# Splits, copies and requests in other orders at seven places of a two-block transformer kernel on one core

## The reference

```python
proj = x @ w_in
q_dsa, c_kv, q_idx, k_idx, w_idx, q_m, k_m, v_m, ga, gb = jnp.split(proj, points, axis=-1)
c_kv = rms_norm(c_kv, kv_norm_g)
k_idx = layer_norm(k_idx, idx_k_norm_g, idx_k_norm_b)
o_a = dsa_attention(q_dsa, c_kv, q_idx, k_idx, w_idx, w_uk, w_uv)
o_b = moba_attention(q_m, k_m, v_m)
merged = sigmoid(ga + b0) * (o_a @ w_o_dsa) + sigmoid(gb + b1) * (o_b @ w_o_moba)
x = layer_norm(ALPHA * x + merged @ w_out)
x = layer_norm(ALPHA * x + mem_cross_attention(x, mem, w_q, w_kv, w_o))
x = layer_norm(ALPHA * x + swiglu(x, w_ffn_in, w_ffn_out))
```

```python
u = depthwise_conv_centred(h2 @ w_up, w_conv, b_conv)
a, v = jnp.split(u, 2, axis=-1)
x = x + gate2 * ((silu(a) * v) @ w_down)
```

## Time and profile before

| | us |
|---|---|
| median of 3 runs (lowest, highest) | 2565.04 (2564.85, 2565.62) |
| the profiled execution | 2564.12 |
| its span, first to last instruction | 2562.5 |
| TensorE busy | 2496.3 (97%) |
| VectorE busy | 1672.0 (65%) |
| ScalarE busy | 1246.3 (49%) |
| GpSimd busy | 106.0 (4%) |
| mean granted TensorE clock | 0.991 |

### The profile page before, as it was taken

How to read it: one execution, slowest core, us unless ns; L and a number is a source line. 1 busy time by engine, 2 the same in 40 slices (tenths; PEclk the granted TensorE clock), 3 DMA queues, 4 the chain that set the end, 5 groups by cost and what they waited for, 6 DMA issues and landing times.

```text
span 2562.5 us, 45817 instructions
## 1 busy us (share of the span) xinstructions
PE 2496.3 (97%) x17896; PEld 2332.3 (91%) x17896; DVE 1672.0 (65%) x2081; ACT 1246.3 (49%) x1582; POOL 106.0 (4%) x149
## 2 busy tenths in 40 slices
PE   7999999999989999999999979999899999999998
PEld 7799999998979999999988878988899999997886
DVE  5564675557867777777777775575666666665556
ACT  4444564444555444444444554544555555554444
POOL 0000000000100000000122000000000000000000
PEclk9999999999999999999999989999999999999999
DMA  7455445569646888888978735446355555555553
GB/s 275 163 183 192 164 147 181 185 230 355 261 167 260 337 343 331 341 334 339 362 287 325 262 121 214 169 158 218 132 195 196 194 188 192 195 198 186 190 196 115
DMA packets 81632, 581.92 MB, mean 227 GB/s; under 512 B 9260, under 2 KB 9420, under 8 KB 11408
## 3 DMA queue, kind: packets, MB, share of 16 engines
q1 hardware_dynamic: 64800, 462.98, 49.3%
q0 software_dynamic: 14464, 104.23, 10.5%
q10 hardware_dynamic: 2288, 13.59, 1.4%
HBM read 578.64 MB, written 2.12 MB: 227 GB/s over the span
## 4 chain that ended last, share of the span: by engine, by line
PE 95%; DVE 3%; ACT 1%; issue 1%; DMA 0%; ACTq 0%; DVEq 0%
PE ps L2005 60%; PE ps L2048 23%; PE ps L2009 7%; PE ps L2072 2%; PE ps L1961 1%; PE ps L2300 0%; DVE xn L1520 0%; PE ps L2146 0%; DVE res L1525 0%; PE ps L2179 0%; PE ps L2191 0%; DVE wlo L1133 0%; DMA xT<-in_xt 0%; DVE res L1664 0%; DVE res L1671 0%
## 5 line engine op out<-in xcount | busy, mean ns | idle before, releaser
L1133 DVE TENSOR_TENSOR wlo<-raw,whi 128x1024 fp32r<-128x1024 f32 x860 | 1041.5, 1227 | 673.8 <-ACT whi L591 670.6
L591 ACT ACTIVATE whi<-raw 128x1024 fp32r<-128x1024 f32 x860 | 901.5, 1061 | 965.6 <-PE ps L2005 596.1
L2005 PE MATMUL ps<-xhi,whi 128*128 128x256 f32 x4176 | 1158.7, 277 | 8.7 <-issue 5.8
L2005 PE MATMUL ps<-xhi,wlo 128*128 128x256 f32 x4176 | 1152.6, 276 | 0.0
L2005 PE MATMUL ps<-xlo,whi 128*128 128x256 f32 x4176 | 1152.4, 276 | 0.0
L2005 PEld LDWEIGHTS ps<-xhi,whi 128*128 128x128 f32 x4176 | 787.3, 189 | 10.9 <-issue 6.7
L2005 PEld LDWEIGHTS ps<-xlo,whi 128*128 128x128 f32 x4176 | 787.2, 188 | 0.4
L2005 PEld LDWEIGHTS ps<-xhi,wlo 128*128 128x128 f32 x4176 | 786.8, 188 | 0.0
L1185 DVE SCALAR_TENSOR_TENSOR ada<-ada,cb 128x2048 f32<-128x2048 f32 x96 | 219.4, 2286 | 4.5 <-DMA ada<-in_w_ada 4.4
L2048 PE MATMUL ps<-whi,dhi 128*128 128x512 f32 x640 | 197.8, 390 | 4.1 <-DVE conv L1899 4.1
L2048 PE MATMUL ps<-whi,dlo 128*128 128x512 f32 x640 | 197.4, 390 | 0.0
(11 more groups left out here) (350 smaller groups left out, 2100.3 us busy)
## 6 DMA issues: line engine op xcount, KB each, us to landing
raw<-in_stream SPq DMA_DIRECT2D x437, 1024.0 KB, 4.8
ada<-in_w_ada POOLq DMA_DIRECT2D x96, 1024.0 KB, 6.8
xT<-in_xt SPq DMA_DIRECT2D x4, 512.0 KB, 10.6
mem_part<-in_memt ACTq DMA_DIRECT2D x2, 1024.0 KB, 7.1
res<-in_x ACTq DMA_DIRECT2D x1, 2048.0 KB, 13.7
gamma<-in_ln_g ACTq DMA_DIRECT2D x2, 1024.0 KB, 11.1
beta<-in_ln_b ACTq DMA_DIRECT2D x2, 1024.0 KB, 15.1
gate_row<-gate_store POOLq DMA_DIRECT2D x2, 1024.0 KB, 6.1
```

Of the source, the lines that this page charges most:

```text
L591: act.activation(whi[:, h % 4], raw[g % 4][:, 1024 * half:1024 * half + 1024], ACT.Copy)\
L1133: dve.tensor_tensor(wlo[:, h % 4], raw[g % 4][:, 1024 * half:1024 * half + 1024], whi[:, h % 4].bitcast(F32), ALU.subtract).then_inc(lo_re ...
L2005: ins = pe.matmul(o, w[:, k, P * m:P * m + P], a(kt), start=begins and n == 0 and m % 2 == 0, stop=ends and n == 2, skip_group_check=True)
```

## The change

Nothing that is computed changes, and no instruction of work is added or removed, but for table loads; the order does.

1. SP waits for a landing before each request of the first tiles: for tile 0's first half ahead of the second quarter of x, and then for the landing before last. ScalarE requests the two constants after it has split tile 1.
2. Tile 6 is split by ScalarE and VectorE ahead of the copies of the transposed latents.
3. ScalarE's attention loop is written out, head by head.
4. TensorE waits for the last two heads only after three half tiles of the first gate product.
5. The first half of `o_mem`'s second tile is split ahead of the heads' copies, and the square root's table is loaded after the last split.
6. In `out2` that table is loaded ahead of the last turn.
7. The first two tiles of `down2` are done in one order of eight steps, `first_two`, which puts t = 1 of tile 0 and of tile 1's first half ahead of t = 0. Tile 1's halves are split one ahead of ScalarE's middle tap and one behind, on VectorE one ahead of the side taps and one behind.

```diff
@@ SP
             sp.dma_start(raw[0][:, D // 2:D], stream[0, :, D // 2:D]).then_inc(raw_landed[0], 16)
+            sp.wait_ge(first_half_landed, 16)
             for s in range(1, 4):
                 sp.dma_start(xT[:, 4 * s:4 * s + 4], xt[:, 4 * s:4 * s + 4]).then_inc(xT_landed[s], 16)
+                sp.wait_ge(xT_landed[s - 1], 16)
                 sp.dma_start(raw[s][:], stream[s]).then_inc(raw_landed[s], 16)
+                sp.wait_ge(raw_landed[s - 1], 16)
@@ ScalarE
             act.dma_start(raw[0][:, 0:D // 2], stream[0, :, 0:D // 2]).then_inc(first_half_landed, 16)
-            act.dma_start(col[:], cols).then_inc(consts_landed, 16)
-            act.dma_start(row[:], rows.partition_broadcast(P)).then_inc(consts_landed, 16)
...
             upper(g0 + 1)
+            act.dma_start(col[:], cols).then_inc(consts_landed, 16)
+            act.dma_start(row[:], rows.partition_broadcast(P)).then_inc(consts_landed, 16)
             for b in range(4, 8):
                 x_first_upper(b)
...
             upper(g0 + 5)
+            upper(g0 + 6)
             act.dma_start(cb[:], c_row.partition_broadcast(P)).then_inc(cb_landed, 16)
             act.wait_ge(small_T, 1)
...
-            for g in range(AT["q_idx"] + 2, AT["q_idx"] + 8):
+            for g in range(AT["q_idx"] + 3, AT["q_idx"] + 8):
                 upper(g + 1)
...
-            with act.Fori(0, 2) as i:
-                for q in range(4):
-                    g = g0 + 2 * q
...
+            for head in range(HEADS):
+                g, q = g0 + 2 * head, head % 4
...
-            def more_upper(name, s):
+            def more_upper(name, s, halves=(0, 1)):
...
             act.dma_start(ln_col[:], ln_cols).then_inc(ln_cols_landed, 16)
+            more_upper("o_mem", 1, (0,))
             for h in range(HEADS_MEM):
                 act.wait_ge(m_o, h + 1)
                 act.activation(shi[:, h], ps[:, 4 + h, 0:S], ACT.Copy).then_inc(shi_ready, 1)
-            sqrt_table()
-            more_upper("o_mem", 1)
+            more_upper("o_mem", 1, (1,))
             more_upper("o_mem", 2)
             upper_of_last("o_mem")
+            sqrt_table()
...
-            sqrt_table()
             for s in range(4):
                 upper(AT["out2"] + s + 1)
...
             later_turns("out2", mixT, 1, 2)
+            sqrt_table()
             last_turn("out2", mixT, 3)
...
             first_turn(hid, dhi)
+            upper(AT["down2"] + 1, halves=(0,))
             middle_tap(1, FC - 1)
             g0 = AT["down2"]
-            upper(g0 + 1)
+            upper(g0 + 1, halves=(1,))
@@ VectorE
             rest(g0 + 5)
+            rest(g0 + 6)
...
             rest(g0 + 4)
+            more_rest("o_mem", 1, (0,))
             for h in range(HEADS_MEM):
...
-            more_rest("o_mem", 1)
+            more_rest("o_mem", 1, (1,))
...
             first_turn("down2", hid, dhi, dlo[1])
-            for s in range(4, 8):
-                beside(s, FC - 1)
-            rests_of_first_turn("down2")
+            rest(AT["down2"] + 1, halves=(0,))
+            beside(4, FC - 1)
+            beside(5, FC - 1)
+            rest(AT["down2"] + 1, halves=(1,))
+            beside(6, FC - 1)
+            for s in range(1, 4):
+                rest(AT["down2"] + s + 1)
@@ TensorE
+            def first_two(g, k, left, reads_of):
+                hi, lo = left
+                steps = [(1, 0, 0), (1, 1, 0), (1, 0, 1), (0, 1, 0), (0, 0, 0), (1, 1, 1), (0, 0, 1), (0, 1, 1)]
+                for n_step, (t, half, s) in enumerate(steps):
+                    h = 2 * (g + s) + half
+                    pe.wait_ge(slo_ready, k + s + 1)
+                    pe.wait_ge(lo_ready, h + 1)
+                    if t == 0 and s == 0:
+                        for c in reads_of:
+                            if c % 2 == half:
+                                pe.wait_ge(pair_read[half], reads(c))
...
+            def heads_beside(half):
+                if half == 2:
+                    pe.wait_ge(att_free, 1 + 2 * HEADS)
+
-            pe.wait_ge(att_free, 1 + 2 * HEADS)
+            pe.wait_ge(att_free, 1 + 2 * 6)
...
-                    chunk(g, c, "T", blocks_in(ohi, olo), 2, 0, i, 16, 3)
+                    chunk(g, c, "T", blocks_in(ohi, olo), 2, 0, i, 16, 3, beside=heads_beside)
```

56 lines of the change are left out of this document (33 added, 23 removed).

## The result

The changed kernel takes 2549.35 us (median of 4 runs, 2548.68 to 2551.00), the kernel before 2564.94 us (4 runs, 2563.03 to 2565.62): ratio 0.9940, 95% interval 0.9929 to 0.9952. It is faster by 15.6 us. The profiled run of the changed kernel took 2548.68 us, its span is 2547.0 us.

A forecast was written before the change was run, and what follows sets the result against it. TensorE, busy 97% of the span, was taken to bound the kernel. Gains of 0 + 2.95 + 1.9 + 1.3 + 1.6 + 0 + 5.4 = 13.15 us gave 2564.1 - 13.15 + 0.9 = 2551.9 us, range 2549.8 to 2556.0 us.

The forecast's parts named there:

- First tiles, 0: Kernel start, changed requests for x, tiles and constants: cost 0, bounds 0.7 us won and 1.0 us lost.
- Index queries 2.95: TensorE's wait for tile 6 goes, as its split now stands ahead of the copies: 2.95 us won.
- attention 1.9: Heads 1 and 5: written out, the table load hides behind the first tile's split, ending TensorE's waits: 1.9 us won.
- gates 1.3: Gates' first product: three half tiles first remove the 1.58 us wait, 0.3 us comes back: 1.3 us won.
- memory heads 1.6: Second tile of the heads' projection: early first-half split, and table load after the last split, end TensorE's wait: 1.6 us won.
- the gates' new wait: Gates, second tile's first half: split ready at 395.2 us but wanted at 394.9 us, so 0.3 us comes back.
- Table load at the second block's output projection, 0: Load moved from behind the Fourier copies to before the last turn; TensorE waits in neither place: cost 0.
- Last projection 5.4: First two tiles: the 4.10 us wait for banks and 1.3 us of lower clock behind it both go: 5.4 us won.
- Rival A: Last projection: tile 1's first split stands ahead of the middle tap, 2.5 of 5.4 us stay: 2554.4 us; chance 0.12.
- Rival B, serial start: Kernel start: SP's waits make tile requests follow one another; 2562.0 us, or 2577.6 us at 7.4 us each; chance 0.04.
- Rival C: New waits behind the four middle places give gains back, 1 us lost at the start: 2560.7 us; chance 0.04.

The follow-up runs named there:

- undone part: The changed kernel with the first tiles as before (SP's waits gone, constants again requested behind ScalarE's first request): 2549.86 us.
- with the clock's part gone: 24 matmuls of zeros put ahead on TensorE: the changed kernel then takes 2549.46 us, the same with the old first tiles 2549.59 us.
- order alone: The changed kernel with tile 1's splits in the last projection at their old places, TensorE's new order kept: 2556.29 us.

## Why the prediction was right or wrong

- *First tiles, 0:* right within its bounds, though one pair of profiles says 0.64 us. The undone part costs 0.04 us, or 0.39 us with the clock's part gone. The first matmul came 0.26 us earlier (bound 0.7). Waits of 0.2 us at the third half tile (where I had 0.4 us of slack) and of 0.5 us at the fifth came in: tile 2's split stands behind ScalarE's wait for x's fourth part, a place I had not worked out. The bounds held.
- *Index queries 2.95, attention 1.9, gates 1.3, memory heads 1.6:* mechanisms right, each too small: 3.19, 2.23, 1.63, 1.71 us. This is the step that failed. The terms were the idle times of the rows, which count from the end of the last matmul; but in a running stream the next one starts long before that end (in the rows of the index queries above, two transposes last 0.38 us together, and the next matmul starts 0.14 us behind the first of them). That overlap is lost too: 2.95 + 0.38 - 0.14 = 3.19 us, just what was measured. It adds 0.13 to 0.29 us to a wait, at five waits 1.0 us, and the gates' new wait shows 0.24 us from start to start in place of 0.3 us idle. With it the sum is 14.2 us, the time 2564.1 - 14.2 + 0.9 = 2550.8 us, and the range reaches down to 2548.8 us. The time measured lies in that range, but still 1.5 us below that sum.
- *Memory heads:* the size was right for a reason given second. The load's move alone is 1.4 to 1.5 us.
- *Table load at the second block's output projection, 0:* right.
- *Last projection 5.4:* right, 5.41 us, the half clock's 1.3 us included. Rival A, a split 1 us late ahead of the middle tap, did not come, and no run makes it; the nearest, order alone, has the split behind the tap and costs 7.1 us.
- *Rival B, serial start:* did not come; with SP's waits x's parts take 6.0 us from request to landing, where they took 10.6 us, and the fourth landed at 19.85 us, 0.9 us later than before.
- *Rival C:* only 0.24 us came back, in the gates, and none in two later profiles of the same gates.
- *The range:* its low end was built from upper bounds of the terms alone and left out that the time itself scatters: the lower clock behind each idle stretch lasts differently in each run, worth over 1 us. Both this and the small terms put 2549.8 us too high; that the first four runs fell below it is in part chance, as nine runs have just that median. Between the terms (14.2 us) and the differences of the medians (15.6 and 15.35 us in the two measurements) over 1 us stays open. All 41 runs of the kernel before on record have a median of 2565.0 us; against the 2549.8 us of nine that is 15.2 us, so 1.0 us over the terms, 0.1 us of it behind the memory heads and 0.0 to 0.4 us the first tiles'. Chance may make the rest, by this scatter, but it isn't shown.

## What to carry to other kernels

Price a wait on TensorE by the distance between the starts around it, less what that distance is in a running stream; its idle time alone is too small. Then add the slow pace behind it. Where an order and a split belong together, test each alone: one of them without the other can be worse than neither. If TensorE must idle for several microseconds, matmuls of zeros in that time bought 4.8 us here, a third of what seven reordered places bought.

## What the runs showed of the hardware

- How many matmuls run at the lower clock behind an idle stretch differs between runs of one kernel: 36 against 26 matmuls in the same 6 us. The Trainium skill (TensorE: Matmul & The Clock Gate, Part 1: The HAM clock gate) says of a kernel's start that this count varies from run to run; the traces agree, with 9 and 18 there in the changed kernel's two profiles.
- A table load of ScalarE starts ahead of the wait that stands before its activation (327.92 us, right behind the read-out, where the changed kernel's copies waited 0.28 us). TensorE lost 0.05 us by it there, and 0.57 us once an activation that carries the wait stood before it. The copies behind it were 1.14 us later in the first case; TensorE could spare some 1.1 us, by the estimate above.
- Zeros count as work for the clock: with 22 matmuls of them, bf16, in the wait, the granted clock in the window behind is 1.00, without them 0.54.
